# Gating the first loads of a two-layer encoder kernel, and moving its first query projection

## The reference, cut to what matters

```python
def even_mixer(h, w_in, w_out, rel_table, lambdas, subln_g, lam_init):
    z = h @ w_in                          # h = rms_norm(x, g), columns 2048
    zf = z[..., :512]                     # Fourier channels
    zq, zk, zv = z[..., 512:1024], z[..., 1024:1536], z[..., 1536:]
    f = fourier_mix(zf)                   # real part of a 2-D DFT
    a = diff_attention(q, k, v, rel_table, lam, lam_init, subln_g)
    return jnp.concatenate([f, a], axis=-1) @ w_out
# layer 0: h += even_mixer(rms_norm(h)); h += swiglu(rms_norm(h))
# layer 1: h += odd_mixer(rms_norm(h));  h += swiglu(rms_norm(h)); final rms_norm
def rms_norm(x, g):
    return x * lax.rsqrt(jnp.mean(x * x, axis=-1, keepdims=True) + 1e-6) * g
```

## Time and profile before

| | us |
|---|---|
| median of 3 runs (1956.31 to 1956.47) | 1956.42 |
| the profiled execution | 1956.4 |
| its longest span, core 0 | 1955.1 |
| the other cores' spans | 1942.3 to 1952.5 |
| TensorE busy on core 0 | 1844.3 (94%) |
| first key projection starts, core 0 | 29.04 |
| first query projection starts, core 0 | 44.04 |
| second group's key projection starts, core 0 | 49.65 |
| first attention matmul, core 0 | 174.54 |

### The profile page before, as it was taken

One profiled execution on the slowest core, in us unless ns is written; L12 is line 12 of the kernel. 1 busy time (PEld: TensorE's weight loads), 2 busy tenths in 40 slices (PEclk: granted clock), 3 DMA queues, 4 the chain that ended last, 5 costly groups with the idle time before them and its releaser, 6 DMA issues.

```text
span 1955.1 us, 36458 instructions; the slowest of 8 cores (1942.3 to 1955.1 us)
## 1 busy us (share of the span) xinstructions
PE 1844.3 (94%) x12742; PEld 1006.1 (51%) x12895; DVE 824.4 (42%) x1751; ACT 891.3 (46%) x1205; POOL 149.6 (8%) x176
## 2 busy tenths in 40 slices
PE   5799999999989998999999999999999999999997
PEld 3576555576556665544444444444444444444443
DVE  3774444555546667722122221324554222221145
ACT  3565778888888887613101113055652131011121
POOL 0000000000000000012100110012041120011100
PEclk8999999999999999999999999999999999999999
DMA  9424211000432001377810654141033976036512
GB/s 227 124 78 72 93 45 35 7 2 7 131 106 86 14 25 40 57 98 106 121 22 14 84 73 63 17 75 34 12 44 46 124 107 81 1 44 86 76 69 105
DMA packets 137056, 129.51 MB, mean 66 GB/s; under 512 B 9777, under 2 KB 116529, under 8 KB 136882
## 3 DMA queue, kind: packets, MB, share of 16 engines
q0 software_dynamic: 112544, 69.22, 26.9%
q1 hardware_dynamic: 24338, 57.96, 9.4%
HBM read 187.97 MB, written 8.39 MB: 100 GB/s over the span
## 4 chain that ended last, share of the span: by engine, by line
PE 81%; ACT 5%; DVE 5%; issue 5%; DMA 3%; SPq 0%; DVEq 0%; ACTq 0%; POOL 0%; POOLq 0%
PE psum L1314 15%; PE psum L1316 15%; PE psum L1337 15%; PE psum L1075 10%; PE psum L1034 6%; PE psum L1476 3%; PE psum L1468 3%; PE psum L919 2%; ACT arena L1058 2%; PE psum L1421 2%; PE psum L829 2%; PE psum L767 1%; DMA arena<-w_in 1%; PE psum L532 1%; PE psum L843 1%
## 5 line engine op out<-in xcount | busy, mean ns | idle before, releaser
L1314 PE MATMUL psum<-arena 128*128 128x512 bf16 x1377 | 329.3, 379 | 3.3 <-DVE arena L1094 1.7
L1320 ACT ACTIVATE arena<-psum 128x512 f32<-128x512 f32 x176 | 104.9, 597 | 498.6 <-PE psum L1314 485.7
L1316 PE MATMUL psum<-arena 128*128 128x512 bf16 x1380 | 330.0, 379 | 1.5
L1075 PE MATMUL psum<-arena 128*128 128x129 bf16 x4096 | 317.6, 221 | 5.7 <-DVE arena L1094 3.4
L1321 DVE TENSOR_TENSOR arena<-psum,arena 128x512 bf16<-128x512 f32 x176 | 121.2, 691 | 454.2 <-PE psum L1316 439.6
L1337 PE MATMUL psum<-arena 128*128 128x512 bf16 x1379 | 305.8, 380 | 1.7 <-issue 0.2
L1075 PEld LDWEIGHTS psum<-arena 128*128 128x128 bf16 x4096 | 252.2, 98 | 104.9 <-issue 77.9
L1056 ACT ACTIVATE arena<-psum 128x1024 bf16<-128x1024 f32 x244 | 242.8, 1022 | 69.7 <-PE psum L1035 64.1
L1316 PEld LDWEIGHTS psum<-arena 128*128 128x128 bf16 x1408 | 137.7, 98 | 166.1
L1314 PEld LDWEIGHTS psum<-arena 128*128 128x128 bf16 x1408 | 137.5, 98 | 164.9 <-issue 1.6
L1337 PEld LDWEIGHTS psum<-arena 128*128 128x128 bf16 x1408 | 137.4, 98 | 162.7 <-issue 2.9
(11 more groups left out here) (125 smaller groups left out, 1644.1 us busy)
## 6 DMA issues: line engine op xcount, KB each, us to landing
arena<-w POOLq DMA_DIRECT2D x88, 512.0 KB, 8.7
arena<-x SPq DMA_DIRECT2D x48, 512.0 KB, 9.5
arena<-w POOLq DMA_DIRECT2D x44, 256.0 KB, 10.4
arena<-dft SPq DMA_DIRECT2D x8, 1024.0 KB, 6.5
out<-arena SPq DMA_DIRECT2D x16, 512.0 KB, 2.7
arena<-wown SPq DMA_DIRECT2D x8, 576.0 KB, 4.4
arena<-wfo SPq DMA_DIRECT2D x8, 512.0 KB, 7.4
arena<-w_uv POOLq DMA_DIRECT2D x4, 1024.0 KB, 15.7
```

Of the source, the lines that this page charges most:

```text
L1075: return lambda: nc.tensor.matmul(psum[:, c0:c0 + 129], lhsT=P_[:, idx * 128:(idx + 1) * 128], rhs=Vp[h // 2][:, kt, h % 2, 0:129], start= ...
L1314: k.group("pe", [(lambda kk=kk: nc.tensor.matmul(bank(b1), lhsT=w13[sl][:, 0, kk, jj * 128:(jj + 1) * 128], rhs=hnT_[:, kk, ts], start=(kk ...
L1316: k.group("pe", [(lambda kk=kk: nc.tensor.matmul(bank(b3), lhsT=w13[sl][:, 1, kk, jj * 128:(jj + 1) * 128], rhs=hnT_[:, kk, ts], start=(kk ...
L1320: k.op("act", lambda: nc.scalar.activation(out=sil[ss_], in_=bank(b1), func=AF.Silu), reads=[bankB[b1]], writes=[silB[ss_]])
```

## The change

The gates of the first loads and the order in group 0 are changed.

```diff
-            k.dma("pool", dst, w_in_d[...], reads={"k": [xtB[0][1]], "v": [xtB[1][1]], "q": []}[nm], writes=[wB[nm]])
+            k.dma("pool", dst, w_in_d[...], reads={"k": [xtB[0][1]], "v": [wB["k"]], "q": [xtB[1][3]]}[nm], writes=[wB[nm]])
             if nm == "k":
-                load_x(1)
+                load_x(1, [gvecB])
...
                 if (n + 2) % 4 == 3 and n // 4 + 2 < 8:
-                    load_x(n // 4 + 2)
+                    load_x(n // 4 + 2, [xtB[1][3]] if n == 1 else ())
...
                 do_tr(4)
                 proj_v(1)
                 do_tr(5)
-                square1(2, 0)
-                square1(2, 1)
+                do_tr(6)
                 proj_q()
                 k.dma("pool", wzT, wzT_d.rearrange("(g p) d -> p g d", p=128), reads=[xtB[0][1]], writes=[wzTB])
-                square1(2, 2)
-                square1(2, 3)
-                do_tr(6)
                 do_tr(7)
+                squares(2)
                 rstd(2)
```

More of the change, by code:

```diff
@@ L398, in build @@
         for nm, dst, c0 in (("k", wk_s, 1024), ("v", wv_s, 1536), ("q", wq_s, 512)):
-            k.dma("pool", dst, w_in_d[:, c0:c0 + 256].rearrange("(k p) c -> p k c", p=128), reads={"k": [xtB[0][1]], "v": [xtB[1][1]], "q": []}[nm], writes=[wB[nm]])
+            k.dma("pool", dst, w_in_d[:, c0:c0 + 256].rearrange("(k p) c -> p k c", p=128), reads={"k": [xtB[0][1]], "v": [wB["k"]], "q": [xtB[1][3]]}[nm], writes=[wB[nm]])
             if nm == "k":
-                load_x(1)
+                load_x(1, [gvecB])
         k.dma("sp", cheb, cheb_d, writes=[constB])
```

## The result

The changed kernel takes 1965.07 us (median of 6, 1963.22 to 1965.76) against 1956.57 of the kernel before (median of 6), a ratio of 1.004 with a 95% interval of 1.0029 to 1.0051: 8.5 us slower. Measured again beside the experiments it was 1.0032 (1.0022 to 1.0043). The forecast was 1959.1 and its range ended at 1964.

What follows compares the result with a forecast made beforehand. TensorE was taken as the bound, with early delays reaching the end one for one. Core 0: 1955.1 - 0.8 (query weights) + 2.5 (squares) = 1956.8, with the clock 1957.8, with 1.3 around it 1959.1 us; range 1953 to 1964.

Steps and rivals of the forecast that it cites:

- What bounds the kernel: Whole kernel: TensorE is 90% busy or more after the second slice; a delay at 50 us reaches the end one for one.
- Key weights, x group 1: First loads: key weights land at 18 to 24, key projection starts 6 us earlier, x group 1 lands at 25; no cost.
- T: Start of the first query projection: before, 44.04 us on core 0, 41.08 on core 7, 39.48 on core 4.
- Query weights: Load before the first query projection: caught beside seven x tiles, it starts at 43.2 on core 0, 0.8 us earlier.
- the slow pace: x packets beside the query weights at 57.5 a microsecond: x lasts to 43.1, the first query projection starts at 44.7.
- the fast pace of x: x packets beside the query weights at 74 a microsecond: x lasts 12.1 us, the first query projection starts at 41.2.
- the middle: Start of core 0's first query projection, taken as 43.2, in the middle of two measured paces of x.
- Squares of group 2: Group 0: all four squares now follow the query evacuation; query projection to transpose 8 grows by 2.48 to 13.87 us.
- The clock: TensorE idles 3.4 us before transpose 8; a fallen clock would cost between 0 and 3.0 us, 1.0 taken.
- The sum: End of the slowest core, core 0, at 1956.8 us, with the clock 1957.8, with 1.3 around it 1959.1.
- rival (b): First stage: x at the slow pace and TensorE's clock falling before transpose 8, costing 3.0; time 1962.7 us, chance 0.25.
- Rival (a): Query weights not caught by x: first query projection at 35 to 36, bound by VectorE; time 1952.0 us, chance 0.13.

Runs made afterwards that it cites:

- x2_after_q: Changed kernel with x group 2 gated on the landing of the query weights instead of x group 1's last tile; ratio 0.9983 to the kernel before.
- q_ungated: Changed kernel with no gate on the query weights, issued right behind the value weights; ratio 1.0002 to the kernel before.
- order_only: Kernel before, its gates kept, with group 0 in the changed order; ratio 1.0015 to the kernel before.
- warm_fill: Changed kernel with 24 matmuls of 256 columns that compute nothing, ahead of transpose 8; ratio 1.0028 to the kernel before.
- q_late: Changed kernel with query weights waiting for x group 2's last tile and the query projections of groups 0 and 1 behind transpose 11; 1948.42 us, ratio 0.9952.
- x1_gate_only: Kernel before with one gate alone, x group 1 waiting for the gain vector; ratio 1.0013 to the kernel before.

## Why the prediction was wrong

**What bounds the kernel: right.** The first stage's delay reached the end one for one. The stretch behind the attention's start is 1778.8 us before and 1777.0 in the changed kernel on the mean of the cores, within what the other kernels show (1776.6 to 1778.8), none of which touches it.

**Key weights, x group 1: right, but for the key projection's start.** The key weights landed at 17.8 on core 0 (18 to 24 was given), x group 1 was in at 24.8 on the mean (25), and the value weights at 28.2 (28). The projection started at 25.1, 2 us later than the 23 of the working: the squares of x group 0, and with them all behind, came 1.3 us later than before on this core. It cost nothing, since T waited for another load.

**Query weights: the step that failed.** The mechanism held, the size did not: the term for their landing beside x, which gave T = 43.2 and at worst 44.7, was too short. T was 47.03 on core 0; 46.16 on core 4 (41.5), 45.34 on core 7 (42.5). I let their packets start with those of x group 2 at 27.5 and go one for one, to 43.1 at the slow pace, with the last 180 through in 0.6 us. Measured on core 6, 59 went from 28 to 32 us, where my 54 a microsecond asked for 216. From 32 to 44 us 901 went, 75 a microsecond, faster than I took, and made up for most of that. x was nearly through at 44, as the slow pace had it. But 102 query packets (119 less 17 in this view from 44 to 47.5 us) were still to go,

```profile
DMA packets 378, 0.61 MB, mean 174 GB/s; under 512 B 17, under 2 KB 119, under 8 KB 378
...
q1 hardware_dynamic: 19, 0.05, 5.5%
```

and they landed at 47.3, 3.3 us later, beside the first packets of wzT, which have 2 KB. T followed after 0.2 us, where I had 1. So core 6 missed the slow sum's 44.7 by 0.9 + 2.7 - 0.8 = 2.8 us. With the 157 packets that the start lacked, all would have been through by 44 (an estimate from these counts): the late start is what left a rest, and the slow rest is what made it cost that much.

The missing part stood in the trace of before: there the key weights were issued at 7.89, and the count of packets from 5 to 12 us, the second line here, has SyncE's queue alone.

```profile
7.89 1.03 POOL L144 DMA_DIRECT2D arena<-w_in  x1 [6.12 <-DMA arena<-x]
```

```profile
q1 hardware_dynamic: 412, 1.50, 96.6%
```

I read the pace of 14 to 20 us and not the wait ahead of it. By the packet records the first query packet comes 4.2 to 5.8 us after the issue on the eight cores of the changed kernel, and at most 1.6 to 2.1 us after it in x2_after_q, with no x group 2 beside it. And in q_ungated, queued ahead of x, the same load lands 5 us earlier or more.

Two readings of the earlier trace rows were off besides. The 520 packets of 35 to 42 us hold 55 of under 512 B, so the fast pace of x was 66 a microsecond and not 74, and the middle would have been 43.7. And the 1582 packets of 25 to 30 us are half of the three weight loads, not nearly all.

**Squares of group 2: right.** 13.87 was forecast for T to transpose 8, 14.1 and 14.0 measured, and order_only has it alone, 13.9.

**The clock: right in kind.** It fell on the six cores that were idle for 3.1 to 3.5 us ahead of transpose 8. On cores 4 and 5 the key projection itself ran partly at half clock (5.35 us on core 4) and left 1.4 us idle; there it did not fall again. Charged 1.0, seen 1.0 (120.2 - 119.2), of which warm_fill gave back 0.3, so that the size is not confirmed.

**The sum and the rivals.** 1959.1 + 3.8 for T on core 0 gives 1962.9; core 6, which lost 6.4 at T (41.1 to 47.5), ended last at 1963.5, with 3.6 us of it from behind the attention's start, where cores differ from one execution to the next. So it went rival (b)'s way (1962.7, chance 0.25), with T beyond its slow pace rather than with a dearer clock; that its time is near comes from two errors that offset each other: T was 2.3 us later on core 0 than (b) had it, and (b) charged 3.0 for the clock. Rival (a) did not come: beside x the weight queue first got 59 packets beside 236 and then 1.2 to 1.3 for each of SyncE's. A rule of the Trainium skill was weighed there (DMA: Bandwidth & Descriptors, section on queues, rings and completion order): the round from queue to queue roughly fits the counts from 32 us on (447 beside 340, 454 beside 388), the 9 to 17 descriptors a turn fit none, and the 59 beside 236 fit neither. The range's upper end was built on the slow pace and is therefore 1 us short.

What stays open is why the first packets come late. That x group 2 holds them is shown by x2_after_q; its first tile was issued 0.3 us ahead of the query weights and the others within 1.4 us behind them, so it is not simply a matter of who came first. How many of its packets go first, and whether it is the engines' or the issuing side's doing, was not measured. Nor was it tried whether the slow rest behind 44 us is the doing of wzT: no run moved wzT alone.

## What to carry to other kernels

A gate that releases two loads with the same event puts them beside each other; if the one with small packets is wanted first, gate the big one on it, or queue the small one ahead. Count the packets of a queue in the stretch behind its issue and in the one ahead of its landing, not only its pace once it flows: here 4.2 to 5.8 us of 19 to 22 passed before the first packet. And before moving a load earlier, move its consumer later: q_late, which did both, gained most.

## What the hardware showed that I had not expected

- A load with 512 B packets, issued on GpSimd at about the time at which x tiles of 4 KB packets are issued on SyncE, hardly starts: 59 packets in 4 us in the changed kernel, 154 in 7 us in x1_gate_only, against 696 in 4 us with no x there.
- A hole in x's stream is worth three times as long beside x: 937 packets in 4 us of x1_gate_only (31 to 35), 454 in 6 us of the changed kernel (38 to 44).
- Cores that start the attention at nearly the same time end up to 9 us apart (from there to the end 1773.4 to 1782.1 us in the profile before), and the time of a program is that of the slowest. A change of a few microseconds was seen more clearly in the mean start of a stage over eight cores than in the time.
